# First modulation of a two-block transformer kernel: w_mod blocks split in two parts for TensorE, five more raw buffers, first key units mixed in

## The reference

```python
silu_c, silu_cc = silu(c), silu(c_ctx)              # one vector each for the tokens and for the context
mod_l = split(silu_c  @ w_mod + b_mod, 6)           # w_mod is 2048 x 12288; six vectors of 2048
mod_c = split(silu_cc @ w_mod + b_mod, 6)           # only its first two are used
hl = rms_norm(x,   norm1_g) * (1 + mod_l[1]) + mod_l[0]
hc = rms_norm(ctx, norm1_g) * (1 + mod_c[1]) + mod_c[0]
zl  = hl @ w_in + b_in                              # queries, keys, values, gates, ...
zkv = hc @ w_in[:, keys and values] + b_in[keys and values]
```

## Time and profile before

| | |
|---|---|
| time, median of three runs | 2849.08 us (2848.26 to 2850.89) |
| time of the profiled execution | 2853.54 us |
| its span | 2851.8 us |
| TensorE busy | 2714.7 us, 95% of the span |
| VectorE, ScalarE, GpSimd busy | 1914.3, 1225.0, 219.7 us |
| DMA | 539.01 MB, mean 189 GB/s |
| granted TensorE clock, mean over the span | 0.975 |

### The profile page before, as it was taken

One profiled execution on the slowest core, in us unless ns is written; L12 is line 12 of the kernel. 1 busy time (PEld: TensorE's weight loads), 2 busy tenths in 40 slices (PEclk: granted clock), 3 DMA queues, 4 the chain that ended last, 5 costly groups with the idle time before them and its releaser, 6 DMA issues.

```text
span 2851.8 us, 51278 instructions
## 1 busy us (share of the span) xinstructions
PE 2714.7 (95%) x21330; PEld 2553.3 (90%) x21330; DVE 1914.3 (67%) x2964; ACT 1225.0 (43%) x1801; POOL 219.7 (8%) x212
## 2 busy tenths in 40 slices
PE   5889999899999899999999999999999998979996
PEld 1279977699999899999999999999999997979996
DVE  5645667789999787875554555677656665477564
ACT  2122244544434544554443444564444444444453
POOL 4000011100003200100000000030000000220011
PEclk8899999999999999999999999999999999989998
DMA  7766643265878687865555555554434443535563
GB/s 252 256 206 236 222 148 116 88 219 160 267 245 256 202 276 258 270 230 195 180 190 183 186 184 187 179 194 155 155 133 158 148 154 110 185 108 177 189 194 110
DMA packets 163991, 539.01 MB, mean 189 GB/s; under 512 B 31024, under 2 KB 35120, under 8 KB 163632
## 3 DMA queue, kind: packets, MB, share of 16 engines
q1 hardware_dynamic: 163760, 535.73, 57.1%
HBM read 533.57 MB, written 2.10 MB: 188 GB/s over the span
## 4 chain that ended last, share of the span: by engine, by line
PE 80%; DVE 14%; issue 2%; DMA 2%; ACT 1%; SPq 1%; POOL 0%; POOLq 0%; ACTq 0%; DVEq 0%
PE ps L479 24%; PE ps L484 24%; PE ps L481 24%; DVE lo L1536 4%; PE ps L580 2%; DVE CV L1796 2%; PE ps L633 1%; PE ps L652 1%; DVE macc L1653 1%; DVE macc L1527 1%; DMA raw<-in_w_mod 1%; DVE macc L1524 1%; PE ps L641 1%; DMA raw<-in_w_in 1%; DVE row L2082 1%
## 5 line engine op out<-in xcount | busy, mean ns | idle before, releaser
L479 PE MATMUL ps<-AH,hi 128*128 128x256 f32 (+2 forms) x4480 | 1284.7, 287 | 13.5 <-DVE AL L2158 13.5
L484 PE MATMUL ps<-AH,lo 128*128 128x256 f32 (+2 forms) x4480 | 1271.8, 284 | 19.1 <-DVE lo L1536 19.1
L481 PE MATMUL ps<-AL,hi 128*128 128x256 f32 (+2 forms) x4480 | 1270.3, 284 | 0.0
L930 ACT ACTIVATE hi<-raw 128x1024 fp32r<-128x1024 f32 x808 | 850.9, 1058 | 929.3 <-PE ps L484 485.0
L1536 DVE TENSOR_TENSOR lo<-raw,hi 128x1024 fp32r<-128x1024 f32 x808 | 977.5, 1224 | 188.9 <-ACT hi L930 186.9
L479 PEld LDWEIGHTS ps<-AH,hi 128*128 128x128 f32 x4480 | 851.0, 190 | 45.5 <-issue 34.6
L484 PEld LDWEIGHTS ps<-AH,lo 128*128 128x128 f32 x4480 | 850.6, 190 | 22.0 <-DVE lo L1536 21.8
L481 PEld LDWEIGHTS ps<-AL,hi 128*128 128x128 f32 x4480 | 851.5, 190 | 0.8
L479 PE MATMUL ps<-YH,hi 128*128 128x256 f32 (+1 forms) x1536 | 434.9, 283 | 6.5 <-DVE YL L2093 6.5
L484 PE MATMUL ps<-YH,lo 128*128 128x256 f32 (+1 forms) x1536 | 434.1, 283 | 0.0
L481 PE MATMUL ps<-YL,hi 128*128 128x256 f32 (+1 forms) x1536 | 433.8, 282 | 0.0
(11 more groups left out here) (245 smaller groups left out, 2606.3 us busy)
## 6 DMA issues: line engine op xcount, KB each, us to landing
raw<-in_w_ff SPq DMA_DIRECT2D x256, 512.0 KB, 4.1
raw<-in_w_in SPq DMA_DIRECT2D x208, 512.0 KB, 4.4
raw<-in_w_mod SPq DMA_DIRECT2D x192, 512.0 KB, 4.5
raw<-in_w_ain SPq DMA_DIRECT2D x128, 512.0 KB, 3.5
raw<-in_w_pin SPq DMA_DIRECT2D x64, 512.0 KB, 3.5
raw<-in_w_o SPq DMA_DIRECT2D x32, 512.0 KB, 4.7
raw<-in_w_aout SPq DMA_DIRECT2D x32, 512.0 KB, 3.5
raw<-in_w_pout SPq DMA_DIRECT2D x32, 512.0 KB, 3.6
```

The lines of the kernel that those rows point to most:

```text
L479: e.matmul(b.ap[:, o], hi[:, k, :], xh, start=start and k + i == 0, stop=False, skip_group_check=many)
L481: e.matmul(b.ap[:, o], hi[:, k, :], xl, start=False, stop=False, skip_group_check=many)
L484: mm = e.matmul(b.ap[:, o], los[j % NSPLIT][:, k, :], xh, start=False, stop=stop and k == KU - 1, skip_group_check=many)
L930: e.activation(his[u % NSPLIT][:, :, :], raws[i % NRAW][:, :].rearrange("p (k m) -> p k m", k=KU), ACT.Copy).then_inc(s_hi, 1)
```

## The change

All 64 blocks of the first modulation now go to TensorE, in the group order MOD0. Of each group, the blocks q = 2 and 5 (WHOLE) are multiplied as before, in float32 ("mod0"). The other six ("mods", 48 in all) are split like ordinary units: hi by ACT, lo by DVE, and PE multiplies each by a stationary operand `CS` of 128 columns, of which four are used (the high and low parts of the two vectors; the others hold zeros or neighbouring vectors, whose rows are not read), with 512 columns moving: four float32r matmuls per block. The results gather in 128 rows of S0 or S1; ACT copies four of them, and the turn adds high and low with the small matrix `comb`. DVE no longer sums any of the 64.

Five more raw buffers exist while the first 68 blocks are loaded; they lie where AH, AL, CH, CL and later tensors are not yet in use. The small input meta is loaded after the second stage instead of early, x after two blocks of w_mod instead of four.

The units of the first key tiles' lower half (w_in 40 to 43, k-tiles 0 to 7) stand in the list at places 48, 53, 58 and 63, between the blocks of the groups 3 and 7. Their upper halves open the second stage. A unit has a `tick()` on PE, but these four have none on ACT and DVE. The modulated tiles come in the order g = 0, 1, 2, 3 instead of 0, 2, 1, 3. The second stage holds 42 of the other w_mod blocks instead of 48; the six move on behind the later ones, which follow at two to five list entries from entry 176 on.

```diff
-MOD_PE, MOD_DVE = (0, 4, 1, 5, 3, 7), (2, 6)
+MOD0 = (0, 4, 1, 5, 2, 6, 3, 7)
+WHOLE = (2, 5)
+NEARLY, NLEAD = 48, 4
+NSTART = 64 + NLEAD
+FIRST = 64 - 8 * len(WHOLE) + NLEAD
+NEXTRA = 5
...
-    on_pe = [("mod0", nb, q) for nb in MOD_PE for q in range(8)]
-    on_dve = [("mod0", nb, q) for nb in MOD_DVE for q in range(8)]
-    for i in range(64):
-        plan.append((on_dve if on_dve and i % 8 in (1, 4, 6) else on_pe).pop(0))
-    for m in list(range(40, 56)) + list(range(32, 40)) + list(range(24, 32)):
+    mod0 = [("mod0" if q in WHOLE else "mods", nb, q) for nb in MOD0 for q in range(8)]
+    plan += mod0[:NEARLY]
+    share = (64 - NEARLY) // NLEAD
+    for j in range(NLEAD):
+        plan.append(("w_in", 40 + j, 0))
+        plan += mod0[NEARLY + share * j:NEARLY + share * (j + 1)]
+    for j in range(NLEAD):
+        plan.append(("w_in", 40 + j, 1))
+    for m in list(range(40 + NLEAD, 56)) + list(range(32, 40)) + list(range(24, 32)):
         full("w_in", m)
-        for _ in range(1 + i % 2 if 64 <= i < 96 else 1 if i >= 176 and i % 5 < 2 + (i % 10 == 9) else 0):
+        for _ in range(1 + i % 2 if NSTART <= i < 96 else 1 if i >= 176 and i % 5 < 2 + (i % 10 == 9) else 0):
...
+        over = ExitStack()
+        extra = []
+        for i in range(2):
+            sb(f"under{i}", [128, 12 * T], F32, over)
+            extra.append(sb(f"raw{NRAW + i}", [128, KU * 128], F32, over))
+            sb(f"beside{i}", [128, 16 * NM], F32, over)
+        over.close()
...
         early, first = ExitStack(), ExitStack()
+        for i in range(2):
+            extra.append(sb(f"raw{NRAW + 2 + i}", [128, KU * 128], F32, first, "right"))
+            sb(f"over{i}", [128, 12 * T], F32, first, "right")
+        first.close()
         CH, CL = (sb(n, [128, 16, T], F32R, early, "right") for n in ("CH", "CL"))
-        mrow = [sb(f"mrow{i}", [2, 512], F32, first, "right") for i in range(2)]
+        mrow = [sb(f"mrow{i}", [4, 512], F32, first, "right") for i in range(2)]
+
+        CS = sb("CS", [128, 192], F32R, first, "right")
+        comb = sb("comb", [128, 2], F32, first, "right")
+        extra.append(sb(f"raw{NRAW + 4}", [128, KU * 128], F32, first))
+        first.close()
+        raws += extra
...
+            b = i % (NRAW + NEXTRA) if i < NSTART else i % NRAW
+            loads[b] += 1
+            raw_at.append(b)
+            load_no.append(loads[b])
+            before.append(last.get(b))
+            last[b] = i
...
+                if before[nxt] is not None:
+                    e.wait_ge(*raw_free[before[nxt]])
+                e.dma_start(raws[raw_at[nxt]][:, :], src).then_inc(s_raw[raw_at[nxt]], 16)
...
+            for _ in range(2):
+                block_in()
             e.dma_start(cst[:, :], ar["cst"]).then_inc(s_cst, 16)
-            for _ in range(NRAW):
+            e.dma_start(H[:, :, NM:L], ar["x"]).then_inc(s_x, 16)
+            for _ in range(4):
                 block_in()
-            e.dma_start(H[:, :, NM:L], ar["x"]).then_inc(s_x, 16)
+            e.dma_start(ctxv, ar["ctx"]).then_inc(s_ctx, 16)
+            for _ in range(NSTART + NRAW - 6):
+                block_in()
+
+            units(32 - NLEAD)
             e.dma_start(H[:, :, 0:NM], ar["meta"]).then_inc(s_meta, 16)
-            e.dma_start(ctxv, ar["ctx"]).then_inc(s_ctx, 16)
-            for _ in range(64):
-                block_in()
-
-            units(32)
...
+            def mod0_turn(r):
                 yield
                 yield
                 opened(xb)
                 e.wait_ge(s_cst, 16)
                 e.wait_ge(s_m0e, r + 1)
                 for j in range(4):
-                    mm = e.matmul(XB[:, 2 * j:2 * j + 2], mrow[r % 2][0:2, 128 * j:128 * j + 128], ident[0:2, 0:2],
+                    mm = e.matmul(XB[:, 2 * j:2 * j + 2], mrow[r % 2][0:4, 128 * j:128 * j + 128], comb[0:4, :],
+                xb.free = (s_m0v, r + 1)
...
+            for i in range(NSTART):
+                name, nb, q = plan[i]
+                if name == "w_in":
+                    b = opened(bank[nb - 40])
+                    unit(b, 0, both, True, False, lambda k: e.wait_ge(s_lx, 2 * k + 2))
+                    continue
+                r = MOD0.index(nb)
+                b = (s0, s1)[r % 2]
+                if q == 0:
+                    opened(b)
+                if name == "mod0":
                     e.wait_ge(*landed(i))
                     for j in range(2):
                         k = 2 * q + j
                         mm = e.matmul(b.ap[0:2, :], vt[:, SC + 2 * k:SC + 2 * k + 2],
-                                      raws[i % NRAW][:, 512 * j:512 * j + 512], start=(k == 0), stop=(k == 15))
+                                      raws[raw_at[i]][:, 512 * j:512 * j + 512], start=False, stop=False,
+                                      skip_group_check=True)
                     mm.then_inc(s_m0p, 1)
-                    if q == 7:
-                        b.free = (s_m0e, on_pe + 1)
-                        spawn(mod0_pe(on_pe))
-                        on_pe += 1
-                elif q == 7:
-                    spawn(mod0_dve(on_dve))
-                    on_dve += 1
+                else:
+                    unit_at += 1
+                    u = unit_at
+                    for part, ready in ((his, s_hi), (los, s_lo)):
+                        w = part[u % NSPLIT][:, :, :].rearrange("p k m -> p (k m)")
+                        e.wait_ge(ready, u + 1)
+                        for j in range(2):
+                            k = 2 * q + j
+                            mm = e.matmul(b.ap[:, :], CS[:, 4 * k:4 * k + 128], w[:, 512 * j:512 * j + 512],
+                                          start=(q == j == 0 and part is his), stop=(q == 7 and j == 1 and part is los),
+                                          skip_group_check=True)
+                    mm.then_inc(s_unit, 1)
+                if q == 7:
+                    b.free = (s_m0e, r + 1)
+                    spawn(mod0_turn(r))
...
             for m in range(16):
-                ready = (lambda k: e.wait_ge(s_lx, 2 * first_k.index(k) + 2)) if m == 0 else None
-                gemm(both, (s_k, m + 1) if m < 8 else (s_vf, m - 7), ready=ready)
+                if m < NLEAD:
+                    unit(bank[m], KU, both, False, True, (lambda k: e.wait_ge(s_lx, 2 * k + 2)) if m == 0 else None)
+                    bank[m].free = (s_k, m + 1)
+                    tile_at = m + 1
+                else:
+                    gemm(both, (s_k, m + 1) if m < 8 else (s_vf, m - 7))
                 if m >= 8:
                     spawn(v_turn(m - 8))
             finish(*ticks.active)
...
+            def first_part(i):
+                u = number_at[i]
+                e.wait_ge(*landed(i))
+                if u >= NSPLIT:
+                    e.wait_ge(s_unit, u - NSPLIT + 1)
+                e.activation(his[u % NSPLIT][:, :, :], raws[raw_at[i]][:, :].rearrange("p (k m) -> p k m", k=KU),
+                             ACT.Copy).then_inc(s_hi, 1)
...
+            def mod0_out(r, nb):
+                e.wait_ge(s_unit, unit_no["mods", nb, 7] + 1)
                 if r > 1:
-                    e.wait_ge(s_m0t, turn_at[MOD_PE[r - 2]] + 1)
-                e.activation(mrow[r % 2][:, :], acc[r % 4][0:2, :], ACT.Copy).then_inc(s_m0e, 1)
-                yield
-                yield
-                have.add(nb)
-                yield
-
-            def mod0_dve(nb):
+                    e.wait_ge(s_m0t, r - 1)
+                e.activation(mrow[r % 2][:, :], SS[r % 2][0:4, :], ACT.Copy).then_inc(s_m0e, 1)
...
+                for g in range(4):
...
+            for i in range(NSTART):
+                name, nb, q = plan[i]
+                if name != "mod0":
+                    first_part(i)
+                if name == "w_in":
+                    continue
                 if q == 7:
-                    spawn(mod0_pe(on_pe, nb) if nb in MOD_PE else mod0_dve(nb))
-                    on_pe += nb in MOD_PE
+                    spawn(mod0_out(MOD0.index(nb), nb))
                 tick()
-            first_parts(-1)
+            first_parts(FIRST - 1)
...
-                units(2)
+                units(1 if m < NLEAD else 2)
...
+            def second_part(i):
+                u = number_at[i]
+                e.wait_ge(s_hi, u + 1)
+                e.tensor_tensor(los[u % NSPLIT][:, :, :], raws[raw_at[i]][:, :].rearrange("p (k m) -> p k m", k=KU),
+                                his[u % NSPLIT][:, :, :].bitcast(F32), ALU.subtract).then_inc(s_lo, 1)
...
+            sc, cs = (a.rearrange("p (k f) -> p k f", k=16) for a in (vt[:, SC:SC + 32], CS[:, 0:64]))
+            e.wait_ge(s_silu, 1)
+            e.tensor_copy(cs[:, :, 0:2], sc).then_inc(*own.up())
+            done()
+            e.tensor_tensor(cs[:, :, 2:4], sc, cs[:, :, 0:2].bitcast(F32), ALU.subtract).then_inc(s_cs, 1)
...
-                for g in (0, 2, 1, 3):
+                for g in range(4):
```

(47 more changed lines are left out.)

98 lines of the change are left out of this document (18 added, 80 removed).

## The result

The changed kernel takes 2866.39 us (median of 4 runs, 2863.44 to 2870.14), the kernel before, run beside it, 2849.74 us (2848.26 to 2850.89): ratio 1.0059, 95% interval 1.0042 to 1.0077. It is slower by 16.7 us, where 12 were predicted. The profiled execution took 2863.44 us, its span 2861.5.

A forecast was written before the change was run, and what follows sets the result against it. The first stage was taken to be bound by ACT, DVE and PE waiting for each other in lockstep. Its start of the second stage, 35.0 us later, less 22.6 of moved TensorE work gave +12.4: 2861 us, range 2840 to 2877.

The forecast's parts named there:

- S: Start of the second stage (its first lo matmul): predicted at 200.9 us, 35.0 later than before.
- x and its norm: Early first stage: x lands at 15.1 us, its squares end at 34.4, its root at 39.7.
- The root of ctx: First stage, end of the norm of ctx: predicted at 71.6 us, against 70.3 before.
- The ties: First stage, engines waiting in turn: 2.2 us per group end, 1.95 per turn, 4.0 us per modulation step beside split blocks.
- T: First lo matmul of block 48, the first early key unit: predicted at 140.2 us, 71.6 plus 68.6.
- A split matmul of 512 columns: TensorE's price for each of a split block's four matmuls: 0.235 us, between 0.213 and 0.43.
- Rival 4: Split matmuls cost as much as float32, 0.43 us each: 2877 us; chance 0.06.
- the stretch from T to the end of block 67: End of the first stage on TensorE: 42.8 us of work, 49.5 with two waits, plus 1.3 for a slow-clock start.
- The tail: Last copy-out to the second stage's start (copy-out, turn, g = 3, lo): 9.9 us, against 10.7 before.
- Rival 2: First stage: engines run ahead of each other, only DVE's own work counts; S = 167.9, 2828 us; chance 0.14.
- Rival 3: First stage: norm of ctx ends much sooner, near 63 us; S = 192, 2853 us, no change; chance 0.14.
- Rival 5: TensorE at 1.2 GHz throughout: S near 247, 2907 us; chance 0.02.

The follow-up runs named there:

- experiment 12: Changed kernel with only the hi of the four early key units made one place ahead of ScalarE's side tasks: 2855.58 us, 1.0011 of the kernel before.
- experiment 1: Changed kernel with ScalarE making hi of each block two list places ahead of its side tasks: 2831.47 us, 0.9939 of the kernel before.
- experiment 2: Changed kernel with four raw buffers instead of nine in the first stage: ratio 1.0099 to the kernel before.
- experiment 3: Changed kernel without the four early key units among the blocks, all key units back in the second stage: 2871.47 us, 1.0076 of the kernel before.
- experiment 7: Changed kernel with hi two places ahead and no early key units among the blocks: 2841.79 us, 0.9972 of the kernel before.
- experiment 8: Changed kernel with all 64 blocks whole on TensorE, keeping nine raw buffers and the four early key units: 2832.86 us, 0.9950 of the kernel before.
- experiment 9: Changed kernel with hi two places ahead and the fourth early key unit moved behind the last block and its turn: 2833.32 us, 0.9948 of the kernel before.
- experiment 11: Changed kernel with hi two places ahead and all 64 blocks split, none whole: 2844.85 us, 0.9984 of the kernel before.

## Why the prediction was right, and where its sizes were off

- **Time = 2849.1 + (S − 165.85) − 22.6** held within 4 us of the medians in twelve kernels (table above). In the terms of this sum S was 5.1 us too small (200.9 against 206.04), and the rest of the sum held.
- **x and its norm**: x was predicted to land at 15.1 us, and ScalarE's first square starts at 15.4. The end of the root of x was predicted for 39.7 and came at 36.94, 2.8 us sooner. Half of that, 1.4, is the wait for block 6, which did not come: its hi started at 26.93 without one. The prediction's end of the squares, 34.4, comes out with four ticks at 2.65 and four at 1.84, where its text suggests six and two; the last square ended at 32.1. The timeline of ScalarE shows the adds with and without a lo beside them:

```profile
28.67 1.04 ACT L960 ACTIVATE hi<-raw 128x1024 fp32r<-128x1024 f32 x1
30.01 0.42 ACT L981 ACTIVATE sqr<-H 128x256 f32<-128x256 f32 x1 [0.30 <-POOL ssum L2284]
31.69 0.42 ACT L981 ACTIVATE sqr<-H 128x256 f32<-128x256 f32 x1 [1.26 <-POOL ssum L2284]
```

An add beside a lo lets the next square start 1.68 us after the last (30.01 to 31.69) where an undisturbed one takes 0.87: 0.81 more, near the lower end of the prediction's bounds, 0.74 to 1.22. The Trainium skill ("SBUF — State Buffer", Who interferes with whom) has a VectorE instruction with two inputs in SBUF and a GpSimd one that reads SBUF contend for an exclusive lock; this trace agrees with an add that waits out what is left of a lo, and not with the tick of 3.0 us that the prediction worked out for full locks.
- **ScalarE stands for TensorE at the end of group 1** until 54.00 (57.1 predicted: 56.1, and 1.0 for TensorE), for 10.21 us. **The root of ctx** ended at 69.0 (71.6 predicted), 2.6 us sooner, about what the root of x was.
- **The ties.** A modulation step takes 3.97 us (4.0 predicted), one beside a whole block 1.57, as predicted (91.09 to 92.66). VectorE waits 2.38 us for hi at two of the group ends (2.2 predicted). They show in ScalarE's timeline, with hi of the next block always right behind mrow, never ahead of it:

```profile
98.66 0.59 ACT L1020 ACTIVATE mrow<-ps 4x512 f32<-4x512 f32 x1 [2.93 <-PE ps L613]
99.16 1.99 ACT L960 ACTIVATE hi<-raw 128x1024 fp32r<-128x1024 f32 x2
...
121.58 0.59 ACT L1020 ACTIVATE mrow<-ps 4x512 f32<-4x512 f32 x1 [2.93 <-PE ps L613]
122.08 3.88 ACT L960 ACTIVATE hi<-raw 128x1024 fp32r<-128x1024 f32 x4
```

From the end of the root to T the sum gave 68.6 us and the trace has 71.9 (69.0 to 140.9). The 3.3 too few come from the waits: VectorE stood for 12.4 us at the four group ends (1.54, twice 2.38, and 6.14 at the last) where 9.2 were put (8.8 less 1.3 hidden, and TensorE's 1.7), and for 6.6 at the three turns (0.46, 2.94, 3.19) where 4.95 were put, three times 1.95 less its own 0.3. Together that is 4.9 more, less the 1.4 that the prediction had added for the clock. The 3.3 us too few here and the 2.6 too many before cancel: T was predicted for 140.2 and came at 140.9. That T agrees so well is luck.
- **A split matmul of 512 columns** was taken at 0.235, between 0.213 and 0.43. TensorE's timeline has hi and lo pairs back to back:

```profile
52.40 0.63 PE L613 MATMUL ps<-lo,CS 128*128 128x512 f32 x2
52.87 0.63 PE L613 MATMUL ps<-hi,CS 128*128 128x512 f32 x2
53.33 0.63 PE L613 MATMUL ps<-lo,CS 128*128 128x512 f32 x2
```

0.465 us a pair, 0.233 each. The Trainium skill's 215.7 ns for 512 columns ("TensorE: Matmul & The Clock Gate", "Wait — 56ns, not 53.3ns?") would be 0.43 a pair; the trace decides for the prediction's estimate, twice the time of 256 columns. Rival 4 is out.
- **The term that was mis-sized** is the stretch from T to the end of block 67: 49.5 + 1.3 = 50.8 us predicted, 55.3 measured (140.90 to 196.17), nearly the whole of the error in S (200.9 against 206.04). TensorE stood for 5.5 of the 55.0 us of the window from 141 to 196 us, where 4.0 + 2.7 were predicted; so the waits are not it, but its busy time is, 49.5 us instead of 42.8. 4.5 us of that are the three falls of the granted clock (experiment 12), for which the prediction had 1.3, one start at the slow clock, because TensorE was granted 0.95 and more where it was always busy. It did not see that stalls here would be followed by 1.5 us at 1.2 GHz, three times. Where the other 2.2 us come from stays open.
- **The tail**: 9.9 us predicted, 9.87 measured. The wait for a w_in block in it went from 1.14 to 0.17.
- **Rival 2** (the engines run ahead of each other) describes the kernel that this change could have been: T near 115 and 2828 us; with hi ahead it is T = 120.4 and 2831.5. It was to decide if the ties cost under 18 us; experiment 1 took out 31.5 us, so they did cost about what the forecast had above rival 2 (200.9 − 167.9 = 33.0).
- **Rival 3** (norm of ctx near 63): it ended at 69.0. **Rival 5** (1.2 GHz throughout): the clock was 0.79 from 69 us up to T and 0.91 behind it.

The change is slower, then, because it makes three engines do each block in turn while each of them has side tasks in program order that wait for another; nine buffers help it by only 5.9 us in the start (experiment 2), since what is missing is mostly not data but an engine that may go on. The version with hi ahead beats both kernels: 0.9939 of before, and by the two ratios some 1.2% less than the change.

## What to carry to other kernels

When work of one engine is handed down a chain of three, look in each engine's program for the operation on which the next block's first step is queued: put that first step ahead of every side task that can wait, before buffers are added. An engine that feeds others should meet its waits after it has fed them; and work that is mixed in early pays only as much as the waits that it really fills, here 4 to 9 us of 22.6 (experiments 3 and 7).

## What the runs showed of the hardware

- TensorE's granted clock fell to 1.2 GHz in dense work after short stalls: also in experiment 8, where it had been busy for 59.88 of 60 us at clock 1.00. There it stood for 1.62 and 0.76 us ahead of and in each of the first two lead units, and matmuls from 107.64 to 110.84 and again from 138.35 to 141.55 started at the slow pace. In the kernel with hi ahead, where the only wait in the lead units was 0.66 us and the longest among the blocks 1.26, it stayed at 1.00 from 90 to 165 us:

```profile
120.00:126.00 6.00, 6.00 (x52) 5.92 (x51) 1.23 (x1) 3.43 (x4) 0.00 (x0) 1.00 0.93 336
132.00:138.00 6.00, 5.37 (x47) 5.37 (x48) 5.84 (x13) 4.10 (x7) 0.00 (x0) 1.00 0.89 339
```

Two stalls of 2.4 us together thus cost 1.5 us more than themselves. One of 1.48 or 1.49 us in a unit, with one of 0.43 to 0.85 just ahead of it, was followed by a fall too (experiments 9, 11 and 12); one of 1.02 (experiment 9) was not. By what rule the clock falls and comes back was not tested.
- With all blocks split (experiment 11) TensorE was granted 0.70 from 69 to 120 us and was busy for 36.3 us of 51; with two of eight whole (experiment 1) it was granted 0.81 and was busy for 43.9. The norm of ctx ends 5.7 us later in the former, so the two windows don't hold quite the same work.
